# Four sections of the modulation product, weighted and summed by GpSimd instead of TensorE

## What is computed

```python
c_act = jax.nn.silu(c)                       # 1 x 1024
for i in range(2):
    mod = c_act @ w_ada[i] + b_ada[i]        # 1024 x 6144 weights per layer
    sh1, sc1, g1, sh2, sc2, g2 = ...         # six sections of 1024 columns
    h = modulate(rms_norm(x, norm_g[i, 0]), sh1, sc1)
    h = s5_mixer(...) if i == 0 else mla_mixer(...)
    x = x + g1 * rms_norm(h, norm_g[i, 1])
    h = modulate(rms_norm(x, norm_g[i, 2]), sh2, sc2)
    h = dense_swiglu(...) if i == 0 else moe_swiglu(...)
    x = x + g2 * rms_norm(h, norm_g[i, 3])
```

## Time and profile before

| | us |
|---|---|
| median of 3 runs | 1075.31 |
| lowest, highest | 1073.29, 1076.22 |
| the profiled execution, its own time | 1072.69 |
| its span in the trace | 1070.9 |
| TensorE busy | 993.8 (93%) |
| VectorE busy | 809.8 (76%) |
| ScalarE busy | 635.7 (59%) |
| GpSimd busy | 46.0 (4%) |

### The profile page before, as it was taken

One profiled execution on the slowest core, in us unless ns is written; L12 is line 12 of the kernel. 1 busy time (PEld: TensorE's weight loads), 2 busy tenths in 40 slices (PEclk: granted clock), 3 DMA queues, 4 the chain that ended last, 5 costly groups with the idle time before them and its releaser, 6 DMA issues.

```text
span 1070.9 us, 17962 instructions
## 1 busy us (share of the span) xinstructions
PE 993.8 (93%) x6758; PEld 823.3 (77%) x6759; DVE 809.8 (76%) x1111; ACT 635.7 (59%) x827; POOL 46.0 (4%) x105
## 2 busy tenths in 40 slices
PE   0786799999999999989999999999999999999995
PEld 0564477888989888767878888888888888888884
DVE  7989785444344646986678888988879888898885
ACT  4436275523342545675477767778677776867763
POOL 3003200000000001001000000000000000000000
PEclk9987799999999999999899999999999999999998
DMA  9898974767868839612369999999999999999971
GB/s 261 300 347 241 246 266 171 252 218 243 298 247 291 309 146 356 214 57 65 115 231 358 337 348 327 333 361 312 347 337 346 339 319 355 319 348 339 332 250 61
DMA packets 192086, 292.99 MB, mean 274 GB/s; under 512 B 11141, under 2 KB 157178, under 8 KB 191754
## 3 DMA queue, kind: packets, MB, share of 16 engines
q1 hardware_dynamic: 185162, 282.92, 76.4%
q10 hardware_dynamic: 4064, 5.26, 1.7%
q0 software_dynamic: 2784, 3.76, 1.7%
HBM read 287.39 MB, written 2.11 MB: 270 GB/s over the span
## 4 chain that ended last, share of the span: by engine, by line
PE 85%; DVE 9%; ACT 3%; issue 2%; DMA 1%; SPq 0%; DVEq 0%; ACTq 0%
PE ps L602 24%; PE ps L604 23%; PE ps L603 23%; PE ps L646 3%; PE ps L1070 3%; PE ps L1107 1%; PE ps L989 1%; PE ps L1096 1%; PE ps L1097 1%; DVE s_out_map L1861 1%; PE ps L691 1%; PE ps L768 1%; PE ps L779 1%; PE ps L758 1%; PE ps L1042 0%
## 5 line engine op out<-in xcount | busy, mean ns | idle before, releaser
L2223 DVE TENSOR_TENSOR w_lo<-raw,w_hi 128x2048 fp32r<-128x2048 f32 x162 | 366.2, 2288 | 64.7 <-ACT w_hi L1570 64.7
L1570 ACT ACTIVATE w_hi<-raw 128x2048 fp32r<-128x2048 f32 x162 | 303.8, 1909 | 0.0
L1654 DVE TENSOR_TENSOR w_lo<-raw,w_hi 128x2048 fp32r<-128x2048 f32 (+3 forms) x59 | 131.6, 2249 | 91.2 <-ACT w_hi L1236 90.2
L602 PE MATMUL ps<-w_hi,xe_hi 128*128 128x512 f32 x448 | 179.2, 400 | 1.3 <-DVE xe_lo L2186 1.3
L604 PE MATMUL ps<-w_hi,xe_lo 128*128 128x512 f32 x448 | 175.4, 392 | 0.0
L603 PE MATMUL ps<-w_lo,xe_hi 128*128 128x512 f32 x448 | 174.8, 390 | 0.0
L1236 ACT ACTIVATE w_hi<-raw 128x2048 fp32r<-128x2048 f32 (+3 forms) x59 | 109.0, 1875 | 70.9 <-DMA raw<-in_ffn_w_in 68.7
L602 PE MATMUL ps<-act_hi,w_hi 128*128 128x256 f32 x352 | 101.1, 287 | 1.9 <-DVE act_lo L1822 1.9
L1578 ACT ACTIVATE e_hi<-ps 128x256 fp32r<-128x256 f32 x56 | 21.5, 385 | 132.1 <-PE ps L1107 132.1
L603 PE MATMUL ps<-act_lo,w_hi 128*128 128x256 f32 x352 | 99.5, 283 | 0.0
L604 PE MATMUL ps<-act_hi,w_lo 128*128 128x256 f32 x352 | 99.5, 283 | 0.0
(11 more groups left out here) (414 smaller groups left out, 1589.5 us busy)
## 6 DMA issues: line engine op xcount, KB each, us to landing
raw<-in_moe_w_in SPq DMA_DIRECT2D x224, 512.0 KB, 5.3
raw<-in_moe_w_out SPq DMA_DIRECT2D x56, 1024.0 KB, 7.5
raw<-in_w_ada SPq DMA_DIRECT2D x48, 1024.0 KB, 9.7
raw<-in_ffn_w_in SPq DMA_DIRECT2D x44, 512.0 KB, 7.7
raw<-in_ffn_w_out SPq DMA_DIRECT2D x11, 1024.0 KB, 10.4
raw<-in_ssm_w_glu SPq DMA_DIRECT2D x16, 512.0 KB, 10.9
raw<-in_mla_w_o SPq DMA_DIRECT2D x4, 1024.0 KB, 8.8
raw<-in_mla_w_uq SPq DMA_DIRECT2D x3, 768.0 KB, 7.8
```

Of the source, the lines that this page charges most:

```text
L602: mm(dst, st[0], mv[0], start=first, stop=False)
L1570: af(HI[:, (V_MOE + m) % RING, :], RAW[:, (RAW_OF_W[V_MOE] + m) % RING, :], cp).then_inc(hi_done, 1)
L1654: tt_(LO[:, slot, 0:w], RAW[:, RAW_OF_W[v] % RING, 0:w], HI[:, slot, 0:w].bitcast(F32), ALU.subtract)\
L2223: tt_(LO[:, slot, :], RAW[:, (RAW_OF_W[V_MOE] + m) % RING, :], HI[:, slot, :].bitcast(F32), ALU.subtract)\
```

## The change

Blocks 28 to 43 (sections 7 to 10) leave TensorE. GpSimd takes each block when it has landed: it multiplies each of its two row blocks by silu(c) of the row, in place in the ring slot (the very first of a section goes into a sum tile `ACC` instead), and adds it to `ACC`. After four blocks `ACC` holds 128 partial sums per column, and TensorE sums the 128 partitions by a product with ones (`ada_total`, four products of 128 x 32 by 128 x 256) at the end of steps 2, 4, 6 and 8. Sections 0 to 6 and 11 stay as they were. The mask semaphore is merged with another one to free a number, which moves nothing.

```diff
+            def ada_weighted(n):
+                s, kk = divmod(n, 4)
+                wait_raw(pool, RAW_OF_ADA[n])
+                pool.wait_ge(ada_used, n)
+                if n == 4 * SUMMED[0]:
+                    pool.wait_ge(n_lo, DT)
+                    pool.memset(ONE32[:, :], 1.0)
+                elif kk == 0:
+                    pool.wait_ge(ada_sum, SUMMED.index(s))
+                for k in range(2):
+                    w = RAW[:, RAW_OF_ADA[n] % RING, k * D:(k + 1) * D]
+                    dst = ACC[:, :] if kk == 0 and k == 0 else w
+                    link_(pool.tensor_scalar(dst, w, CB[:, 2 * kk + k, 0:1], None, ALU.mult))
+                    if dst is w:
+                        ins = pool.tensor_tensor(ACC[:, :], ACC[:, :], w, ALU.add)
+                        if k == 0:
+                            link_(ins)
+                ins.then_inc(ada_used, 1)
...
             for s in range(7, NSEC):
                 section_rows(s)
+                if s in SUMMED:
+                    for n in range(4 * s, 4 * s + 4):
+                        ada_weighted(n)
                 if s - 1 in GATES:
                     gate_store(s - 1)
...
+            def ada_total(s):
+                pe.wait_ge(ada_used, 4 * (s + 1))
+                pe.wait_ge(wide_ok, s - 1)
+                if s - 2 not in GATES:
+                    pe.wait_ge(mod_ok, sum(1 for i in range(s - 1) if i not in GATES))
+                for c4 in range(4):
+                    last = mm(PS[32 * c4:32 * c4 + 32, ada_bank(s), 0:256], ONE32[:, :], ACC[:, c4 * 256:(c4 + 1) * 256],
+                              start=True, stop=True)
+                last.then_inc(ada_sum, 1)
...
                 if t:
                     ffn_down(t - 1)
-                for n in range(26 + 2 * t, 26 + 2 * t + (ADA_PER_STEP(t) if t else 0)):
-                    ada(n)
+                if t % 2 == 0 and 6 + t // 2 in SUMMED:
+                    ada_total(6 + t // 2)
...
             def wide(s):
-                act.wait_ge(ada_used, 4 * (s + 1))
+                act.wait_ge(*((ada_sum, SUMMED.index(s) + 1) if s in SUMMED else (ada_used, 4 * (s + 1))))
```

More of the change, by code:

```diff
@@ L53 @@
 GATES = (2, 5, 8, 11)
+SUMMED = (7, 8, 9, 10)
 TWO_PI_1 = 6.28125
@@ L184, in program @@
         RES_END = at("res_tmp_end", [P, TT, D], 48 + 8 * ((V_ALL - 5) % RING))
+        ACC = at("ada_acc", [P, D], 152)
         WIDE = at("ada_wide", [P, 2, 256], 196)
@@ L241, in program @@
         IOTA = at("iota", [P, P], kc + 2.625)
+        ONE32 = at("ones_32", [P, 32], 156)
         IOTI = nc.alloc_sbuf_tensor_at("iota_i", [P, P], I32, offset=BASE + int(142 * KB))
@@ L278, in program @@
             "vec_ps vec_ok ldt_ok at_ps ct_ps ct_ok cact_ok cb_ok")
-        wide_ok, mrow_ok, mod_ps, mod_ok, gate_in, mask_ok = sems("wide_ok mrow_ok mod_ps mod_ok gate_in mask_ok")
+        wide_ok, mrow_ok, mod_ps, mod_ok, gate_in, ada_sum = sems("wide_ok mrow_ok mod_ps mod_ok gate_in ada_sum")
         dch, ach, pch = sems("dve_chain act_chain pool_chain")
@@ L578, in _ @@
             pool.affine_select(out=MASK[:, P:], in_=MASK[:, P:], compare_op=ALU.is_ge, fill=NEG, base=0,
-                               pattern=[[-1, P]], channel_multiplier=1).then_inc(mask_ok, 1)
+                               pattern=[[-1, P]], channel_multiplier=1).then_inc(tri_ok, 1)
             pool.wait_ge(o_mm, H)
@@ L1045, in _ @@
             keep_warm(3, 7)
-            pe.wait_ge(tri_ok, 1)
+            pe.wait_ge(tri_ok, 2)
             pe.wait_ge(msk_ok, 1)
@@ L2093, in _ @@
                 v_.tensor_copy(VV[:, 1, 4 * b:4 * b + 4, :], kv[:, :, NOPE:]).then_inc(kv1_ok, 1)
-            dve.wait_ge(mask_ok, 1)
+            dve.wait_ge(tri_ok, 1)
             dve.wait_ge(q_rope, 2)
```

## The result

The changed kernel takes 1123.3 us (median of 4 runs, 1123.1 to 1123.5) against 1075.4 for the kernel before (4 runs, 1073.3 to 1076.2). The ratio is 1.045, 95% interval 1.043 to 1.047: **48 us slower**. The direction was forecast, the size was not: 1089 was predicted, with a range that ended at 1110.

What follows compares the result with a forecast made beforehand. TensorE alone bounded the loop; GpSimd would set the new pace. Section 7 at -2.9 and steps 3 to 8 at +16.1 gave +13.2 on 1072.7, so 1085.9, plus 2.6 for the median: 1088.5, given as 1089; range 1061 to 1110.

Steps and rivals of the forecast that it cites:

- What bounds the kernel before: Loop steps 3 to 8: TensorE alone, busy the whole window; without its removed products two steps take 35.3 us.
- The price of the multiplication: GpSimd, 128x1024 by a column: 1.2 us, between 0.95 from the MEMSET slope and 1.7 from the CAST.
- The addition, 2.4: GpSimd addition of two 128x1024 tiles: 2.4 us, twice the multiplication, between 1.23 and 5.1.
- The exclusion: GpSimd stands still while DVE subtractions run, and the reverse: 15.4 us in two steps, about 1 us off under DMA issues.
- section 7: First section on GpSimd: done at 240.9, step 3 starts at 241.5, -2.9 us.
- Section 10: Last section on GpSimd: its rows wait for section 8's gate store, cycle 45.7 us against 43.0.
- Ones-products: TensorE's four `ada_total`, at the ends of steps 2, 4, 6 and 8: 0.47 us each, 1.9 in all.
- Edits at nothing: Loop: earlier or equal slot release for units A, ACT's wait for the total, DVE's delayed subtractions; all counted as no cost.
- A: Loop: the engines don't exclude each other, GpSimd hides wholly, -13.0 us, result 1062.3; chance 0.16.
- B: GpSimd sections: exclusion but cheap operations, 0.95 and 1.9 us, result about 1071.6; chance 0.12.
- C: GpSimd sections: exclusion and dear operations, 1.7 and 3.4 us, result about 1132; chance 0.12.
- D: TensorE's clock falls after gaps, costing up to some 5 us behind the last total; inside the range, no separate chance.

Runs made afterwards that it cites:

- the better kernels: Changed kernel with GpSimd taking two of four blocks: first of each step with cheap or dear multiplication, or blocks 0 and 1, cheap, before the rows; 1069.1, 1068.8, 1069.2 us.
- the kernel with two blocks: Changed kernel with GpSimd taking only blocks 0 and 1 of each section, TensorE blocks 2 and 3, multiplication form unchanged; 1074.6 us, ratio 1.000.
- the second try with spare products: Changed kernel with 28, 52, 56 and 74 spare 128x128 products on TensorE ahead of its four waits for the sums; 1123.0 us, ratio 1.044.

## Why the prediction was wrong, step by step

**What bounds the kernel before: right.** With GpSimd's part cut down the cycle is 35.4 us, where I had worked out 35.3 from the products; with DVE's part cut down in the kernel before nothing changes.

**The price of the multiplication: the step that failed.** I took 1.2 us with an upper end of 1.7, and it is 2.85. "Nearer the MEMSET, because its slope comes from one operation at two lengths" was the choice: but a MEMSET reads nothing (in one of the experiments it took 0.96 for 128 x 1024, the very slope), and the CAST that gave the upper end stood in one row of 128 columns. Neither was a bound: 2.85 lies above both, and no row of the trace before shows this operation. I had also ordered the two operations by the number of tiles they read; the trace has it the other way round, 2.85 against 2.40. It is 8 x 1.65 = 13.2 us a section. **The addition, 2.4, was right**, though by a rule (twice the multiplication) that is wrong. The Trainium skill (GPSIMD Engine Reference, "Elementwise — side-by-side cycle accounting") has 4497 ns for an addition of 2048 columns, which gives an estimate of 2.25 for it; the 2.40 supports that within 7%.

**The exclusion: right in kind, too large.** I had 14.4 us net a section; 9.2 is what cycle less own work gives, and 9.0 to 9.2 a cycle is what the run without `w_lo` gave back. I let DVE and GpSimd stand still for each other over the whole of every operation. A multiplication in this form holds DVE only in its first 0.9 us or so (260.58 to 261.4), and a `w_lo` that comes later runs beside it at no cost to either. The 1.0 us that I took off for a `w_lo` under the row issues is in no row, either: it begins at 243.74, when both issues are through the earlier trace rows, and in the changed kernel none runs beside the issues (248.73 to 249.82; the `w_lo` before it ends at 241.23, the next begins at 256.24). Of the Trainium skill's rule (SBUF — State Buffer, "SBUF: two separate sides" and "Who interferes with whom": whichever of the two starts first has the shared ports for the whole instruction, and the other blocks) this case shows the additions, and the two-tensor multiplication, to agree, and the multiplication by a column not to: 280.67 to 282.96 beside 279.01 to 281.86, both undisturbed.

**How the two errors add up.** With 2.85 in my sum and nothing else changed, a cycle is 56.2, 56.2 and 58.9 us (+55.7 over the three), section 7 ends 10.1 us later than before, and the result is 1141. What was measured is 17.9 less: 4.7 in section 7, 13.2 in the cycles. This is a difference, and the terms account for it. In the cycles I had 3 x (14.4 - 9.2) = 15.6 us of exclusion too much, against 3 x 0.4 for own work that is 42.2 and not 41.8, and 1.1 for section 10: 13.3. In section 7 GpSimd takes 51.8 us from its first multiplication to its last addition (196.95 to 248.79), 10.7 above its own work, where I had 16.3; 0.3 more of own work and 0.6 more for the ones-product leave 4.7. In my own terms: section 7 came out at +5.4 us where I had -2.9, the three cycles at +42.5 where I had +16.1. So the direction was right, and the forecast of 1089 was nearer than its price deserved, because the two errors had opposite signs.

**Section 10: right.** I had 2.7 us more for it than for the others and it took 3.8; the experiment that moves the store takes 3.4 of them away.

**Ones-products: 0.61 us, not 0.47**, and 1.08 at the lower clock level (1.2 GHz; granted clock 0.67 from 240 to 251 us). I had scaled the 1.86 by the number of products. It matters nothing behind a wait, and 0.6 us in all for the better kernels.

**Edits at nothing: right here.** DVE's `w_lo` grew from 2.29 to 4.3 us where an addition was ahead, but TensorE had 7 to 18 us to spare, and no gap came at the start of a step, which my signs had tied to a `w_lo` of over 4 us. It was not nothing in the kernel with two blocks, where TensorE waited 4.5 us for a split.

**The rivals.** A (no exclusion) falls with the timelines and with the 36 us. B (cheap operations) falls with 2.85. C had the region (1132), but with the wrong operation made dear: 38.6 us own work of which the additions at 3.4 are the larger part, against 41.1 with the multiplications the larger. That it came so near was luck. My range left it out at a chance of 0.12, though its prices, 1.7 and 3.4, I had worked out from rows myself. D (the clock) has no more than the 2.8 us that are left of the 50.7 behind step 9. From 406.9 to 411 us the granted clock is 0.50, then 1.00, so an estimate from the rows is half of these 4 us, 2.0. No run takes it away: in the second try with spare products the clock fell behind the last total, too.

## What to carry to other kernels

A price for an operation that the trace does not show must not be narrowed to the friendlier of its bounds: carried through the sum, the ends gave 1072 and over 1132, and the range had to hold both. And a bound that comes from another operation is a guess, too: 2.85 lay above the upper one. One run with the very operation, even in a loop cut to a few columns, would have shown that it is the dear one (0.44 us against 0.32 for the addition at 64 columns). Before elementwise work goes to GpSimd, compare its own time, undisturbed, with the time of the stage that is to hide it, and leave room for a quarter to a third more where VectorE works on SBUF beside it as here (9.2 us on 42.2, 11.9 on 34.5); where it does not fit, a share of it may: half of the blocks hid wholly and gained 4.0 to 4.6 us, near the 5.0 that they took from TensorE. And the form of the operation is worth a look, since the same product cost 2.85 us in one and 1.89 in the other, and 20 us of the kernel's time.

## What was not expected of the hardware

- On GpSimd, 128 x 1024 in float32: a MEMSET 0.96 us, a product of two tensors with the second a repeated column 1.89, an addition of two tensors 2.40, a product with one factor per partition 2.85, with a constant 2.78. The one with a single input tile of this width is the dearest; why, no run shows.
- The product with a factor per partition holds VectorE's two-input operations back for its first 0.9 us or so, the two-tensor operations until their end. So the cheaper form cost VectorE more: its `gt_lo`, 0.42 us alone, took 1.13 on average in the changed kernel and 1.84 with the two-tensor product.

The two groups of DVE between 197 and 400 us, of the changed kernel and of that with the two-tensor product:

```profile
L2060 DVE TENSOR_TENSOR gt_lo<-ffn_prod,gt_hi 128x256 fp32r<-128x256 f32 x18 | 20.4, 1133 | 4.8 <-ACT gt_hi L1479 4.8
```

```profile
L2060 DVE TENSOR_TENSOR gt_lo<-ffn_prod,gt_hi 128x256 fp32r<-128x256 f32 x18 | 33.2, 1843 | 4.8 <-ACT gt_hi L1479 4.8
```

- An addition on GpSimd held back operations of VectorE with one input tile as well: in the changed kernel a product on 128 x 32, whose like take 0.18 us beside it, began 0.20 us into the addition of 404.51, took 2.20 and ended at 406.91, with the addition ending at 406.87.
- TensorE's clock was at its lower level behind each of the four waits of 7.68 to 17.70 us (ones-products at 1.08 us, the products behind them at 0.41 instead of 0.28). In the run with spare products it was there behind the wait of 4.05 us, stayed at the upper level behind those of 1.44 and 1.98, and behind the one of 3.51 fell only 0.9 us after the engine had begun to work again. Holding it up behind two of the four totals did not change the time by more than the measurement tells.
